# Tile 1 of the prompt: time mixing in halves beside the expert gathers, which begin with tile 0 alone

## What is computed

```python
def step(S, inp):
    r_t, d_t, k_t, v_t, kk_t, a_t = inp
    Skk = jnp.einsum('bhvk,bhk->bhv', S, kk_t)
    S = (S * d_t[:, :, None, :]
         - Skk[..., None] * (kk_t * a_t)[:, :, None, :]
         + v_t[..., None] * k_t[:, :, None, :])
    y_t = jnp.einsum('bhvk,bhk->bhv', S, r_t)
    return S, y_t
```

```python
eidx = jnp.take_along_axis(cand_i, top_pos, axis=-1)
gate = jax.nn.softmax(top_s, axis=-1)
u = expert_u[eidx].astype(F32)
h = jax.nn.gelu(jnp.einsum('nhkd,nd->nhk', u, xr.astype(F32)), approximate=False)
out = jnp.einsum('nhk,nhkd->nd', gate * h, expert_v[eidx].astype(F32))
```

## Time and profile before

| | us |
|---|---|
| median of 3 runs (3208.02 to 3220.68) | 3212.05 |
| the profiled execution | 3226.92 |
| its span, first to last instruction | 3225.1 |

### The profile page before, as it was taken

The page is one execution under the profiler, slowest core; times in us unless marked ns, Lnnn a source line. Parts: engine busy times, 40 slices in busy tenths (PEclk is TensorE's granted clock), DMA queues, the critical chain, the costliest instruction groups (busy, mean ns, idle before and its releaser), DMA issues. The chain is left out here.

```text
span 3225.1 us, 33248 instructions
## 1 busy us (share of the span) xinstructions
PE 2134.7 (66%) x11625; PEld 1139.7 (35%) x11625; DVE 1785.9 (55%) x4126; ACT 674.9 (21%) x1920; POOL 1062.9 (33%) x990
## 2 busy tenths in 40 slices
PE   6949668482487686758567675577766666745555
PEld 3428557271144353423224322234223342512222
DVE  2043353237785765576665764846844445775555
ACT  1022121010221321111331112511212222111111
POOL 0003122003265463334333324333332233334442
PEclk9979788695688697879778788887887888967777
DMA  5230200345889999999999999999999999979998
GB/s 174 90 137 1 80 1 18 115 123 231 339 308 374 358 357 396 420 396 405 410 362 420 388 402 416 357 409 420 383 414 419 411 420 399 408 290 421 420 420 336
DMA packets 152820, 1019.55 MB, mean 316 GB/s; under 512 B 17872, under 2 KB 18944, under 8 KB 37456
## 3 DMA queue, kind: packets, MB, share of 16 engines
q0 software_dynamic: 117024, 825.84, 64.0%
q1 hardware_dynamic: 35632, 191.58, 15.1%
HBM read 992.71 MB, written 18.39 MB: 314 GB/s over the span
## 5 line engine op out<-in xcount | busy, mean ns | idle before, releaser
L1328 PE MATMUL fl_acc<-fl_pairs,fl_diag 128*64 128x512 f32 x2576 | 822.0, 741 | 477.3 <-ACT fl_diag L1301 458.2
L1355 POOL DMA_INDIRECT fl_pairs<-in_peer_uv,fl_row_at x644 | 734.8, 1141 | 1151.5 <-PE fl_acc L1328 1028.7
L1281 DVE CUSTOM_DVE_ANT_0 fl_pairs<-fl_pairs,fl_rows 128x1024 f32<-128x1024 f32 x644 | 785.0, 1238 | 427.8 <-DMA fl_pairs<-in_peer_uv,fl_row_at 426.7
L1328 PEld LDWEIGHTS fl_acc<-fl_pairs,fl_diag 128*64 128x64 f32 x2576 | 280.3, 161 | 891.4 <-issue 844.8
L1307 ACT ACTIVATE fl_acts<-fl_dots 128x2 f32<-128x2 f32 x384 | 77.8, 203 | 1270.6 <-DVE fl_dots L1281 1254.1
L1301 ACT ACTIVATE fl_diag<-constants_sb,fl_mix 128x64 f32<-128x64 f32 x768 | 223.8, 341 | 295.9 <-DVE fl_mix L1271 286.0
L1328 PE MATMUL fl_acc<-fl_more,fl_diag 128*64 128x512 f32 x496 | 172.4, 791 | 102.7 <-ACT fl_diag L1301 86.1
L1355 POOL DMA_INDIRECT fl_more<-in_peer_uv,fl_row_at x124 | 144.3, 1164 | 249.8 <-PE fl_acc L1328 227.8
L1281 DVE CUSTOM_DVE_ANT_0 fl_more<-fl_more,fl_rows 128x1024 f32<-128x1024 f32 x124 | 150.0, 1225 | 88.9 <-DMA fl_more<-in_peer_uv,fl_row_at 88.6
L1786 PE MATMUL aacc<-pc_ring,at_xT 128*128 128x512 f32 x288 | 140.8, 632 | 12.6 <-PEq L1713 12.6
L284 PE MATMUL acc<-w_ring,mixed 128*128 128x512 f32 x288 | 125.7, 598 | 10.0 <-issue 9.1
(11 more groups left out here) (509 smaller groups left out, 2904.3 us busy)
## 6 DMA issues: line engine op xcount, KB each, us to landing
pc_ring<-in_kvq_by_pair SPq DMA_DIRECT2D x36, 1024.0 KB
pc_ring<-in_query_by_head SPq DMA_DIRECT2D x32, 1024.0 KB
pc_ring<-in_past_k SPq DMA_DIRECT2D x16, 1024.0 KB
pc_ring<-in_past_v SPq DMA_DIRECT2D x16, 1024.0 KB
w_ring<-in_rwkv_w_rkv SPq DMA_DIRECT2D x24, 512.0 KB, 3.4
pc_ring<-in_out_by_pair SPq DMA_DIRECT2D x12, 1024.0 KB
fl_pairs<-in_peer_uv,fl_row_at POOLq DMA_INDIRECT x644
fl_pairs<-in_query_by_head SPq DMA_DIRECT2D x8, 1024.0 KB, 10.1
```

The costliest lines, as they stand in the source:

```text
L1281: dve.tensor_tensor_reduce(pair, pair, self.rows[:, u % 2, j, :], 1.0, 0.0, ALU.mult, ALU.add, self.dots[:, u % 2, q, j:j + 1]).then_inc(* ...
L1328: mm = pe.matmul(self.acc[j * FOLD:(j + 1) * FOLD, half, :], self.diag[:, self.summed % self.DIAGS, j, :], self.pair(g)[:, D + half * HALF ...
L1355: pool.indirect_dma_start(self.pair(g), None, self.io["peer_uv"], bass.IndirectOffsetOnAxis(ap=self.row_at[:, u % TILES, j, q:q + 1], axis ...
```

## The change

The serial part computes tile 0 only: one pass of the `wkv_` stages, one tile in `project_and_norm`, and `open_flow` with 128 columns instead of 256, without the scores of tile 1. The gathers start after it; `open_flow` ends at turn 2 instead of 14. Tile 1 goes through `mixing_tile` in halves, with turns 2 to 61 beside it; its own `Pieces` load the projection and query weights. The sample tile follows with turns 61 to 127, and the choice for tile 1 beside its first two stages (indices written at tick 20 and read at tick 22 of the first `half_chunks`). The turns of each stage:

| stages | before | after |
|---|---|---|
| `open_flow` | 14 | 2 |
| mixing of tile 1: operands, chunks, outputs, the same again | none | 4, 15, 6, 4, 15, 6 |
| features, projection, features, scores | none | 1, 3, 1, 4 |
| mixing of tile 2: operands, chunks, outputs, the same again | 5, 20, 8, 5, 20, 8 | 2, 13, 7, 4, 17, 7 |
| features, projection, features, scores | 1, 6, 1, 12 | 1, 5, 1, 9 |
| attention tile 0 (its first three stages) | 65 (4, 2, 14) | 54 (1, 1, 11) |
| attention tile 1 | 65 | 60 |
| attention tile 2 | 80 | 67 |
| the end | 74 | 76 |

`plan` gets a limit: the turns never pass those of the units whose indices have been read (`self.turned`). `NARROW` becomes gathers 0 to 239, since the two more places are opened only at the sample tile's projection.

```diff
@@ -1177,7 +1165,7 @@
 
 
     PLACES, KEPT, DIAGS = 10, 8, 5
-    NARROW = range(24, 176)
+    NARROW = range(0, 240)
 
     def __init__(self, core, io, ctx):
         def sb(name, shape, dt=F32):
@@ -1225,13 +1214,19 @@
         self.start = len(self.dots_by)
         gelu_lag, mix_lag, diag_lag, sum_lag = lags
         for n in range(1, self.ticks + 1):
-            due = self.first + (self.last - self.first) * n // self.ticks
+            for u, _, in_at in turn:
+                if in_at == n - 1:
+                    self.turned = u + 1
+            due = max(self.dots_by[-1], min(self.first + (self.last - self.first) * n // self.ticks, self.turned * TURNS))
             back = lambda k: due if k == 0 else self.dots_by[-k] if k <= len(self.dots_by) else 0
             mixes = max(self.mixes_by[-1], min(back(mix_lag), self.gelus_by[-1]))
             diags = max(self.diags_by[-1], min(back(diag_lag), mixes, self.sums_by[-1] + self.DIAGS))
             sums = max(self.sums_by[-1], min(back(sum_lag), diags))
             while due > self.dots_by[-1] and not self.room(due, sums):
                 due -= 1
+            if n == self.ticks:
+                for u, _, in_at in turn:
+                    self.turned = max(self.turned, u + 1 if in_at in (n, n - 1) else 0)
             self.gelus_by.append(max(self.gelus_by[-1], min(back(gelu_lag), due)))
             self.dots_by.append(due)
             self.mixes_by.append(mixes)
...
@@ -1391,14 +1386,15 @@
 
     PLACES = 4
 
-    def __init__(self, core, io, ctx):
+    def __init__(self, core, io, ctx, t):
         self.core = core
-        self.ring = ctx.enter_context(core.nc.sbuf_tensor("pc_ring", [P, self.PLACES, 2 * D], F32, side="right"))
+        self.ring = ctx.enter_context(core.nc.sbuf_tensor(f"pc_ring_{t}", [P, self.PLACES, 2 * D], F32, side="right"))
         flat = lambda x: x.rearrange("p a b -> p (a b)")
         self.sources, self.first, self.freed, self.loaded = [], {}, {}, 0
+        self.came = [core.lasting(f"piece_in{i}_{t}") for i in range(self.PLACES)]
         self.expect("mix", [flat(io["mix_by_pair"][k]) for k in range(KD // 2)])
         self.expect("query0", [flat(io["query_by_head"][0, i]) for i in range(PH)])
-        for t in range(TILES):
+        for t in range(TILES if t == 2 else 0):
             self.expect(f"kvq{t}", [flat(io["kvq_by_pair"][n]) for n in range(3 * KD // 2)])
             if t == 2:
                 past = {n: [flat(io[f"past_{n}"][i // 2, i % 2]) for i in range(2 * DEC_BATCH)] for n in "kv"}
...
@@ -1521,18 +1515,17 @@
 
 
 
-    HC, RING, WIDTH = 2 * PH, 4, SEQ
+    HC, RING, WIDTH = 2 * PH, 4, P
     nc, choice = core.nc, flow.choice
     with ExitStack() as ctx:
         def sb(name, shape):
...
@@ -1546,7 +1539,6 @@
             @block.gpsimd
             def _(pool):
                 flow.spread_rows(pool, 0)
-                flow.spread_rows(pool, 1)
                 flow.turn_rows_out(pool, 0)
                 flow.turn_rows_in(pool, 0)
                 for n in range(1, last + 1):
...
@@ -1604,16 +1592,8 @@
                     drain(choice.best_of(dve, choice.scores, q))
                 drain(choice.rest(dve, 0))
                 choice.softmax(dve, 0)
-                dve.wait_ge(*s_done.at(len(order)))
-                group, q = None, 0
                 for n in range(1, last + 1):
                     flow.vector(dve, n)
-                    if 2 <= n < last and (n - 2) % 3 == 0 and q < HC // 4:
-                        group, q = choice.best_of(dve, scores1, q), q + 1
-                    if group is not None:
-                        advance(group, 7)
-                    if (n - 2) % 3 == 2 and group is not None:
-                        drain(group)
         core.end_stage()
 
 
@@ -2964,7 +2944,6 @@
     pairs = iter(at)
     with ExitStack() as ctx:
         gated = ctx.enter_context(nc.sbuf_tensor(f"mt_gated_{t}", [P, D], F32))
-        flow.close_extra()
         for part in range(2):
             with ExitStack() as of_half:
                 x = HalfTile(core, of_half, t, part)
@@ -2974,8 +2953,9 @@
                 half_chunks(core, flow, x, last, **events)
                 last, events = next(pairs)
                 half_outputs(core, io, flow, x, carry, gated, last, **events)
-        flow.open_extra()
-        pieces = Pieces(core, io, later)
+        if t == 2:
+            flow.open_extra()
+        pieces = Pieces(core, io, later, t)
         with ExitStack() as proj:
             mixT = proj.enter_context(nc.sbuf_tensor(f"mt_T_{t}", [P, KD, P], F32))
             last, events = next(pairs)
@@ -3082,9 +3062,13 @@
             rwkv_projections(core, io, buf)
         if stages == 1:
             return
+        core.x_tok = ctx.enter_context(nc.sbuf_tensor("x_tok", [P, TILES, D], F32))
+        neg_lam = ctx.enter_context(nc.sbuf_tensor("neg_lam", [P, 1], F32))
+        carrying = ExitStack()
+        carry = carrying.enter_context(nc.sbuf_tensor("carry", [P, H // 2, N], F32))
         with ExitStack() as wkv:
-            w = {"carry": wkv.enter_context(nc.sbuf_tensor("carry", [P, H // 2, N], F32))}
-            for t in range(TILES - 1):
+            w = {"carry": carry[:]}
+            for t in range(1):
                 with ExitStack() as per_tile:
...
@@ -3105,20 +3089,18 @@
                         wkv_outputs(core, io, tile, w, t)
         if stages == 2:
             return
-        core.x_tok = ctx.enter_context(nc.sbuf_tensor("x_tok", [P, TILES, D], F32))
         with ExitStack() as rwkv:
-            gated = rwkv.enter_context(nc.sbuf_tensor("gated_wkv", [P, TILES - 1, D], F32))
-            mixT = rwkv.enter_context(nc.sbuf_tensor("mixT", [P, KD, SEQ], F32))
-            load_rows(core, io, gated, TILES - 1)
-            to_features(core, gated, mixT, "rwkv", TILES - 1)
-            project_and_norm(core, io, mixT, io["mix_by_pair"], 0, "rwkv", TILES - 1)
-        neg_lam = ctx.enter_context(nc.sbuf_tensor("neg_lam", [P, 1], F32))
+            gated = rwkv.enter_context(nc.sbuf_tensor("gated_wkv", [P, 1, D], F32))
+            mixT = rwkv.enter_context(nc.sbuf_tensor("mixT", [P, KD, P], F32))
+            load_rows(core, io, gated, 1)
+            to_features(core, gated, mixT, "rwkv", 1)
+            project_and_norm(core, io, mixT, io["mix_by_pair"], 0, "rwkv", 1)
         mixing_weight(core, io, neg_lam)
-        experts_and_attention(core, io, ctx, neg_lam)
+        experts_and_attention(core, io, ctx, carrying, carry, neg_lam)
         stores_done(core)
...
@@ -3129,27 +3111,31 @@
 
     nc = core.nc
     flow = Flow(core, io, ctx)
-    flow.open_extra()
     with ExitStack() as early:
-        xT = early.enter_context(nc.sbuf_tensor("peer_xT", [P, KD, SEQ], F32))
-        to_features(core, core.x_tok, xT, "peer0", TILES - 1)
-        open_flow(core, io, flow, xT, 14)
+        xT = early.enter_context(nc.sbuf_tensor("peer_xT", [P, KD, P], F32))
+        to_features(core, core.x_tok, xT, "peer0", 1)
+        open_flow(core, io, flow, xT, 2)
+    with ExitStack() as later:
+        mixing_tile(core, io, flow, 1, carry, later, [
+            (6, {}), (21, {}), (27, {}), (31, {}), (46, {}), (52, {}), (53, {}), (56, {}), (57, {}), (61, {})])
+    carrying.close()
     later = ExitStack()
     pieces = mixing_tile(core, io, flow, 2, None, later, [
-        (19, dict(choose=1, side=25)), (39, dict(side=50, end=18, turn=((1, 21, 24),))), (47, {}), (52, {}), (72, {}), (80, {}), (81, {}), (87, {}), (88, {}), (100, {})])
+        (63, dict(rows=((1, 1),), choose=1, side=25)), (76, dict(side=50, end=18, turn=((1, 20, 22),))), (83, {}), (87, {}), (104, {}), (111, {}),
+        (112, {}), (117, {}), (118, {}), (127, {})])
     with ExitStack() as prompt:
         kT = prompt.enter_context(nc.sbuf_tensor("at_kT", [P, DH, SEQ], F32))
         v_tok = prompt.enter_context(nc.sbuf_tensor("at_v", [P, 2, D], F32))
         attention_tile(core, io, flow, pieces, 0, neg_lam, kT, v_tok, [
-            (104, dict(rows=((2, 1),), choose=2, side=20)), (106, dict(side=20)), (120, dict(side=50, end=9, turn=((2, 11, 13),))), (126, {}),
-            (138, {}), (142, {}), (148, {}), (151, {}), (165, {})])
+            (128, dict(rows=((2, 1),), choose=2, side=20)), (129, dict(side=20)), (140, dict(side=50, end=9, turn=((2, 11, 12),))), (146, {}),
+            (156, {}), (160, {}), (166, {}), (168, {}), (181, {})])
         attention_tile(core, io, flow, pieces, 1, neg_lam, kT, v_tok, [
-            (169, dict(rows=((3, 1),), choose=3, side=20)), (171, dict(side=20)), (185, dict(side=50, end=9, turn=((3, 11, 13),))), (191, {}),
-            (203, {}), (207, {}), (213, {}), (216, {}), (230, {})])
+            (184, dict(rows=((3, 1),), choose=3, side=20)), (185, dict(side=20)), (198, dict(side=50, end=9, turn=((3, 11, 12),))), (204, {}),
+            (216, {}), (220, {}), (226, {}), (228, {}), (241, {})])
     attention_tile(core, io, flow, pieces, 2, neg_lam, None, None, [
```

(6 more changed lines are left out.)

48 lines of the change are left out of this document (16 added, 32 removed).

## The result

The changed kernel takes 3311.03 us, median of 4 runs (3310.93 to 3315.16), where the kernel before, beside it, took 3214.32: a ratio of 1.031, interval 1.029 to 1.0325. The profiled span is 3313.4 us against 3225.1, 88.3 longer. The forecast was 3215.

The account below looks back on a forecast made before the run. A serial part, then gathers paced by engines in the mixing and by transfers later. Stages sum 526+13+450+511+399+407+549+373 = 3228 us of span against 3225.1; that +3 on the median gives 3215, range 3125 to 3300.

Parts of the forecast that it names:

- the serial part: Work ahead of the first gather: 233 us removed, so the first gather goes from 759.5 to about 526.
- transfers would not pace the mixing: Tile 1's mixing: 59 turns and all loads, some 143 MB, carried in 450 us at 318 GB/s, costed at nothing.
- the second joint: Attention tile 0, where tile 2's indices come late: 147 us for 13 turns, together about 399 against 417.6.
- the 12 us that I laid on top for tile 1's read: Attention tile 1: turn 192 becomes known when 191 are planned, so the ring drains: plus 12 (0 to 20).
- the late start of tile 1's gathers: Sample tile's first chunk stage: gathers wait for tile 1's indices, 118 us (bounds 100 and 140), before 123.9.
- 12 turns need 60 us at 5.0, in two bursts of four: Sample tile's first chunk stage, behind the late index read: 12 turns at 5.0 us, in bursts since the ring has 8 places.
- the joints are longer: Rival, both late index reads: slower ticks and bursts without overlap, sum 73 us, span 3301, median 3288; chance 0.20.
- The clock rival: Rival, tile 1's chunk stages: TensorE's granted clock falls to 0.65, twice 39 us more, span 3306, median 3293; chance 0.04.
- the price of tile 1's chunk stages: Tile 1's mixing, two chunk stages of 15 turns: 98 us each (bounds 93 and 105), at 2.15 us of PE per turn.
- the division by 0.87: Tile 1's chunk stages: 85 us of PE work taken as 87% of the stage, giving 98 us.
- The outputs stages: Tile 1's mixing, two outputs stages: 48 us each, from 58.6 with 8 turns, at some 2.8 us per turn left out.
- Ring of 8, nothing: Ring of gathered rows with 8 places up to gather 239, 10 before outside gathers 24 to 175: nothing (0 to 10 us).

Follow-up runs that it names:

- Spread: Changed kernel with the turns behind a late index read spread evenly over the ticks left; ratio 1.0225 to the kernel before, sample tile's first chunk stage 131.1 us.
- quiet: Changed kernel with no turn beside tile 1's mixing and its 59 turns alone behind it; the mixing took 311.8 us, the 59 turns 301.6.
- turns20: Changed kernel with 20 turns instead of 15 in each chunk stage of tile 1, at ticks 2, 4, 6, 7, fewer in its lighter stages; 3328.19 us.
- grace: Changed kernel with late turns spread evenly, the first due only 3 ticks (5 in attention) after the index read; ratio 1.0232 to the kernel before.
- phase246: Changed kernel with the 15 turns of tile 1's chunk stages at ticks 2, 4, 6 of each seven, not 3, 5, 7; ratio 1.0376 to the kernel before.
- combo: Changed kernel with the edits of grace and turns20, plus idle TensorE products in tile 1's outputs stages; ratio 1.0228 to the kernel before.

## Why the prediction was wrong

Right were: the serial part (first gather 528.88, forecast 526); that transfers would not pace the mixing (302 GB/s, forecast 310 to 318); the sum of projection, features and scores beside the second load of weights (101.1 us of tile 1, forecast 95); the second joint (attention tile 0 400.3, forecast 399); and about what a turn left out of attention tiles 1 and 2 returns, 23.0 us for 5 and 57.5 for 13, 4.4 to 4.6 each where 5.0 was forecast (the 12 us that I laid on top for tile 1's read were not there). The sample tile's second chunk stage took 102.8, forecast 103: the price of a turn held where the stage was like the one it came from.

Wrong was first **the late start of tile 1's gathers**, "118 us (bounds 100 and 140)" for the sample tile's first chunk stage, 158.9 measured. Three of its numbers failed. The index write came at 53 us and not 42; that DVE's ticks wait for PE there (17.5 us for hc_x alone in the stage) is in the rows, that it is the whole reason is not shown. From write to first dot were 16 us, not 12.5: POOL read the indices back behind three instructions of the mixing. And "12 turns need 60 us at 5.0, in two bursts of four" took the transfers as the pace; a turn was 8.2 us in the bursts, since ring, dots and mixing waited for each other. Spread shows it: with the same late read and the bursts gone, 28 of the 41 us come back.

The rival "the joints are longer" had this place and this mechanism, at 20 us for the ticks and 15 for the bursts. It gave 3301 for the span and I gave it 0.20. That it came near 3313.4 is in part luck, as it also had 30 us at the second joint, which went as forecast. The clock rival's 3306 is nearer by luck alone: its fall did not happen.

Wrong was second **the price of tile 1's chunk stages**: 98 each (bounds 93 and 105), measured 110.6 and 114.4. PE's work was right, 87.7 and 91.6 us against 85. The failed step is the division by 0.87: PE was busy 79 and 80% of the stage. I took the price from a stage with 20 turns at ticks 2, 4, 6, 7 and thought it a price per turn; it is a price per turn at a tick. With turns at 4, 6, 7 the same stage takes 102.1 and 105.6, about my upper bound. PE's idle time is waits in the written chain, 13.7 us of it for hc_x behind the dots of tick 3, and no share of 0.87 foresees that.

Without a turn the stage takes 68.9 us, where 52.8 / 0.87 = 61 was implied, PE being busy 57.4.

Smaller: the operands stages, 34 and 29 forecast, took 43.6 and 38.5. There DVE waits for a small load, ho_vec: 9.5 and 8.8 us, and 1.9 in the stage of before from which I took the price. Why it lands later isn't shown: quiet, with no gathers, waited 4.4 us, and the stage of before had more traffic (344 GB/s) than these (303 and 274).
The outputs stages, 48 forecast, took 39.9 and 38.4: six turns cost 11.0 us there over quiet's 28.9, 1.8 each and not 2.8, and gave back 18. "Ring of 8, nothing" cost perhaps 11. The clock rival had its fall in the wrong stages: the chunk stages were granted 0.91 and 0.87, and where the clock plainly mattered was the outputs stages of the experiments, most in turns20.

Three slips in the forecast's working are small: 42, 12.5 and 60 are 114.5 and not 118, 147 and 254 are 401 and not 399, and three turns, not two, lie ahead of the late read (61 to 64).

The range of 3125 to 3300 ended 11 us too low. All bounds of the joint and of the chunk stages at their upper ends (140 and twice 105) would have given 22 + 14 = 36 more than the forecast, 3251: the terms were too narrow, not only their sum.

## What to carry to other kernels

When work is moved so that a choice is made later than its first use, count how many units are in hand at the joint, and price what comes behind it by the slowest loop (buffer, wait, use), not by the transfer rate; spreading the late units over what is left gave back 28 of 46 us. Moving the choice earlier, or holding units back for the second joint, gave nothing, since choice and units stand in the same engine's queue. And look in the trace whether an edit of a schedule changed the order of instructions where it was meant to: in spread and grace, at the second joint, it had not, and an unchanged time there answers nothing. A unit of work inserted into a chain between engines has no price of its own: the same 15 turns cost 35, 44 or 49 us in one stage, by the tick at which they stood. Take such a price from a stage with the same places, or measure the stage with none.

## What the runs showed of the hardware

A dot product of 1.22 us on VectorE took up to 4.3 us (3.70 above, 4.34 in phase246) when GpSimd was multiplying 128x512 tiles beside it: all 20 long dots of 254 ended 1.07 to 1.10 us behind such a multiplication, and the issue of a gather alone stretched none of 89. And adding some 28 products that nothing reads made two stages of turns20 6.5 to 6.8 us shorter, with the granted clock going from 0.64 to 0.87 and 0.85; in combo one of the same two stages gained nothing, at 0.77.
